# Odd mixer of a two-layer block: the last convolution chunk on VectorE instead of TensorE

## What is computed

```python
def sparse_attn_conformer_mixer(h, ...):
    u = h @ w_in
    ...
    o_nsa = native_sparse_attention(...)        # 8 heads of 64, 256 tokens
    a, b = jnp.split(cf, 2, axis=-1)            # 512 channels each
    z = a * jax.nn.sigmoid(b)
    z = causal_dwconv(z, conf_dw) + conf_dw_b   # depthwise, 31 taps over time
    z = jax.nn.silu(layer_norm(z, conf_ln_g, conf_ln_b))
    return jnp.concatenate([o_nsa, z], axis=-1) @ w_out
```

## Time and profile before

| | us |
|---|---|
| median of 3 runs | 1068.94 |
| lowest and highest run | 1055.47, 1072.68 |
| profiled execution, its own time | 1060.81 |
| its span in the trace | 1059.0 |
| PE busy, share of the span | 95% |
| DVE busy, share of the span | 59% |
| granted TensorE clock, mean | 0.982 |

### The profile page before, as it was taken

How to read it: one execution, slowest core, us unless ns; L and a number is a source line. 1 busy time by engine, 2 the same in 40 slices (tenths; PEclk the granted TensorE clock), 3 DMA queues, 4 the chain that set the end, 5 groups by cost and what they waited for, 6 DMA issues and landing times.

```text
span 1059.0 us, 16632 instructions
## 1 busy us (share of the span) xinstructions
PE 1010.6 (95%) x6822; PEld 902.1 (85%) x6822; DVE 620.1 (59%) x817; ACT 495.5 (47%) x723; POOL 198.6 (19%) x183
## 2 busy tenths in 40 slices
PE   5999999999998999999999999999999999699998
PEld 5988999999797789799999997777777778699996
DVE  4755554554688678665444546555755555646664
ACT  5346344344544443563344346454445544445452
POOL 0005950000222140000000001605253306200100
PEclk9999999999999699999999999999999999899999
DMA  8554665556584130346565564545453536263361
GB/s 270 191 179 145 211 199 170 190 194 195 144 257 160 49 112 2 99 154 190 194 198 170 189 236 143 175 127 166 128 190 122 158 105 200 80 199 119 110 210 40
DMA packets 120418, 168.69 MB, mean 159 GB/s; under 512 B 6372, under 2 KB 89508, under 8 KB 120356
## 3 DMA queue, kind: packets, MB, share of 16 engines
q1 hardware_dynamic: 119920, 167.65, 49.1%
q10 hardware_dynamic: 436, 0.19, 0.1%
HBM read 165.36 MB, written 2.46 MB: 158 GB/s over the span
## 4 chain that ended last, share of the span: by engine, by line
PE 88%; DVE 4%; ACT 3%; POOL 2%; issue 2%; DMA 1%; SPq 0%; DVEq 0%; ACTq 0%; POOLq 0%
PE ps L410 25%; PE ps L411 24%; PE ps L412 24%; PE ps L773 3%; PE ps L761 2%; PE ps L747 2%; PE ps L447 1%; PE ps L591 1%; ACT scratch_sb L811 1%; PE ps L457 1%; PE ps L450 1%; DVE wlo_sb L399 1%; PE ps L824 1%; DMA scratch_sb<-conf_dw 1%; POOL b_inv_sb L2204 1%
## 5 line engine op out<-in xcount | busy, mean ns | idle before, releaser
L399 DVE TENSOR_TENSOR wlo_sb<-raw_sb,whi_sb 128x2048 fp32r<-128x2048 f32 x150 | 345.7, 2306 | 201.2 <-ACT whi_sb L393 201.2
L393 ACT ACTIVATE whi_sb<-raw_sb 128x2048 fp32r<-128x2048 f32 x150 | 287.1, 1915 | 172.9 <-PE ps L412 161.2
L410 PE MATMUL ps<-hhi_sb,whi_sb 128*128 128x256 f32 x1024 | 289.4, 283 | 9.3 <-DVE qkl_sb L2090 7.2
L411 PE MATMUL ps<-hlo_sb,whi_sb 128*128 128x256 f32 x1024 | 287.6, 281 | 0.0
L412 PE MATMUL ps<-hhi_sb,wlo_sb 128*128 128x256 f32 x1024 | 287.3, 281 | 0.0
L410 PEld LDWEIGHTS ps<-hhi_sb,whi_sb 128*128 128x128 f32 x1024 | 194.4, 190 | 12.0 <-DVE wlo_sb L399 7.4
L411 PEld LDWEIGHTS ps<-hlo_sb,whi_sb 128*128 128x128 f32 x1024 | 194.5, 190 | 0.9
L412 PEld LDWEIGHTS ps<-hhi_sb,wlo_sb 128*128 128x128 f32 x1024 | 194.3, 190 | 0.0
L410 PE MATMUL ps<-whi_sb,hhi_sb 128*128 128x512 f32 (+1 forms) x304 | 120.2, 395 | 0.0
L410 PE MATMUL ps<-whi_sb,yhi_sb 128*128 128x512 f32 (+1 forms) x288 | 113.7, 395 | 3.4 <-issue 2.8
L412 PE MATMUL ps<-whi_sb,hlo_sb 128*128 128x512 f32 (+1 forms) x304 | 116.6, 383 | 0.0
(11 more groups left out here) (304 smaller groups left out, 1417.9 us busy)
## 6 DMA issues: line engine op xcount, KB each, us to landing
raw_sb<-w_in SPq DMA_DIRECT2D x45, 1024.0 KB, 5.2
raw_sb<-ffn_gate SPq DMA_DIRECT2D x22, 1024.0 KB, 5.3
raw_sb<-ffn_up SPq DMA_DIRECT2D x22, 1024.0 KB, 5.3
raw_sb<-ffn_down SPq DMA_DIRECT2D x22, 1024.0 KB, 4.9
raw_sb<-w_in_odd SPq DMA_DIRECT2D x9, 1024.0 KB, 5.2
raw_sb<-w_in_even SPq DMA_DIRECT2D x8, 1024.0 KB, 7.1
raw_sb<-w_branch SPq DMA_DIRECT2D x6, 1024.0 KB, 5.1
scratch_sb<-bias_rows_dram SPq DMA_DIRECT2D x40, 128.0 KB, 2.9
```

The lines of the kernel that those rows point to most:

```text
L393: nc.scalar.activation(whi[:, n0 % SPLIT, :], raw[:, n0 % RAW, :], ACT.Copy).then_inc(hi_ready, 1)
L399: nc.vector.tensor_tensor(wlo[:, n0 % SPLIT, :], raw[:, n0 % RAW, :], whi[:, n0 % SPLIT, :].bitcast(F32), ALU.subtract).then_inc(lo_ready, 1)
L410: nc.tensor.matmul(dst, l_hi, r_hi, start=first, stop=False)
L411: nc.tensor.matmul(dst, l_hi, r_lo, start=False, stop=False)
```

## The change

All 31 taps of chunk 3 go to DVE. The list of `conf_taps` now alternates between chunks 2 and 3 as it does between 0 and 1, with 4 taps at every step from 14 on. The products of `conv3` on PE, the splits of z for it on ACT and DVE, the diagonals on POOL, the splits of the tap weights (L2308, L2413) and `conv3_rest` are gone. PE's wait ahead of `channel_mean` is now for all 124 taps.

```diff
-PE_TAPS = 28
...
-        CONF_STEP, Z_STEP, ZH_STEP, ZL_STEP = (12, 13), 14, 15, 16
+        CONF_STEP, Z_STEP = (12, 13), 14
...
-                if m in CONV3_STEP:
-                    k = 2 * CONV3_STEP.index(m)
-                    if k == 0:
-                        pe.wait_ge(z_ready, 4)
-                        pe.wait_ge(z3_lo, 1)
-                        pe.wait_ge(diag_ready, 2 * PE_TAPS)
-                    conv3((k, k + 1))
...
-            pe.wait_ge(conf_step, 3 * CONF_K)
-            pe.wait_ge(conv3_step, CONF_K - PE_TAPS + 1)
+            pe.wait_ge(conf_step, 4 * CONF_K)
             channel_mean(zc, T)
...
-                    k, c = (s // 2, s % 2) if s < 2 * CONF_K else (s - 2 * CONF_K, 2)
+                    k, c = s % (2 * CONF_K) // 2, s // (2 * CONF_K) * 2 + s % 2
...
-                        dve.wait_ge(conf_step, s if c == 2 else s - 1)
+                        dve.wait_ge(conf_step, s - 1)
...
-                if m == ZL_STEP:
-                    dve.wait_ge(z3_hi, 1)
-                    nc.vector.tensor_tensor(zl, zp[:, 3, :], zh.bitcast(F32), ALU.subtract).then_inc(z3_lo, 1)
...
-                if m == CONV3_REST:
-                    conf_taps(3 * CONF_K, 3 * CONF_K)
-                    conv3_rest()
                 if m not in LO_STEP:
-                    conf_taps(2 if m % 2 == 0 else 3, (2 if m < Z_STEP else 3) * CONF_K)
+                    conf_taps((2 if m % 2 == 0 else 3) if m < Z_STEP else 4, (2 if m < Z_STEP else 4) * CONF_K)
...
-            for k in range(PE_TAPS):
-                nc.gpsimd.tensor_scalar(dgh[k], ident[:, :], dwh[:, k:k + 1].bitcast(F32), None,
-                                        ALU.mult).then_inc(diag_ready, 1)
-                nc.gpsimd.tensor_scalar(dgl[k], ident[:, :], dwl[:, k:k + 1].bitcast(F32), None,
-                                        ALU.mult).then_inc(diag_ready, 1)
```

More of the change, by code:

```diff
@@ L155, in build @@
         kcTl = sb("kcTl", [P, 16], F32R)
-        dwh = sb("dwh", [P, PE_TAPS], F32R)
-        dwl = sb("dwl", [P, PE_TAPS], F32R)
         gwhi = sb("gwhi", [P, KC, 24], F32R)
@@ L296, in build @@
         unit_r, hide_r = (t[:, :, :].rearrange("p k n -> p (k n)") for t in (gwhi, gwlo))
[L299 to L305, removed]
         bias_dram = nc.dram_tensor("bias_rows_dram", (H_TOT, SKEW_ROWS, DREL), F32, kind="Internal").ap()
@@ L354, in build @@
         hide_set = sem("hide_set")
-        dw_hi, dw_lo, diag_ready, z3_hi, z3_lo, conv3_done, conv3_step = (
-            sem("dw_hi"), sem("dw_lo"), sem("diag_ready"), sem("z3_hi"), sem("z3_lo"), sem("conv3_done"),
-            sem("conv3_step"))
         kv_twice, rot_ready, roped, kc_roped, kc_heads_T, u_scaled = (
@@ L897, in build @@
         FIN_STEP, OC_SUM_STEP, SUM_STEP, OT_STEP = (18, 30), (22, 31), 26, 31
-        GROUP_STEP, CONV3_REST = (8, 16, 24), 30
-        STEPS1, CONV3_STEP = range(-2, 33), range(17, 31)
+        GROUP_STEP = (8, 16, 24)
+        STEPS1 = range(-2, 33)
         def mix1_pe(pe):
@@ L969, in out_rows @@
                 mm_rows(n, yhi, ylo, k0, first, last).then_inc(tile_used, 1)
[L971 to L976, removed]
             def cmp_part(row, k0, k1):
@@ L1203, in mix1_act @@
                         pair_copy_act(act, jobs1, 0, p, 0, 2)
[L1204 to L1207, removed]
                 if m in HID_STEP:
@@ L2271, in _ @@
             pool.wait_ge(ident_landed, 16)
-            pool.wait_ge(dw_hi, 1)
-            pool.wait_ge(dw_lo, 1)
-            pool.wait_ge(x_added, 4)
-            for k in range(PE_TAPS):
-                nc.gpsimd.tensor_scalar(dgh[k], ident[:, :], dwh[:, k:k + 1].bitcast(F32), None,
-                                        ALU.mult).then_inc(diag_ready, 1)
-                nc.gpsimd.tensor_scalar(dgl[k], ident[:, :], dwl[:, k:k + 1].bitcast(F32), None,
-                                        ALU.mult).then_inc(diag_ready, 1)
             norm_pool(pool, 2)
@@ L2306, in _ @@
                                          ps[:, t, :], ACT.Copy).then_inc(c_copied, 1)
-            act.wait_ge(half_set, 1)
-            nc.scalar.activation(dwh[:, :], dwv[:, 0:PE_TAPS, 3], ACT.Copy).then_inc(dw_hi, 1)
             act.wait_ge(pool_mm, 1)
@@ L2411, in _ @@
             split_lo(dve, N_MIX0 + 10)
-            dve.wait_ge(dw_hi, 1)
-            nc.vector.tensor_tensor(dwl[:, :], dwv[:, 0:PE_TAPS, 3], dwh[:, :].bitcast(F32),
-                                    ALU.subtract).then_inc(dw_lo, 1)
             gate(1)
```

## The result

The changed kernel takes 1073.34 us in the median of 20 runs (1067.51 to 1080.44); the kernel before, on the same chip, takes 1059.96 us in the median of 20 (1053.73 to 1077.3). The ratio is 1.0131, with a 95% interval of 1.0111 to 1.0150: slower by 12 to 16 us. The forecast of the time, 1075 us, lay close for a poor reason: its base, the median of three runs, was 9 us too high, and its effect, +6 us, was about half of the least that the change costs and less than half of the 13 to 14 us measured. Two errors of opposite sign met; that is luck.

A forecast was written before the change was run, and what follows sets the result against it. The prediction took PE to bound the stage, DVE next; DVE's queue (+3 us) and a low clock over one long pair (+3 us) gave +6 us on the 1068.9 us median, so 1075 us, range 1060 to 1084 us.

The forecast's parts named there:

- the third case: Clock stays low from 388 us to the stage's end and PE is the bound again: +12 us, chance 0.15.
- the first: Forecast case: DVE's queue sets the stage (+3 us), clock low over one long PE pair (+3 us): +6 us, chance 0.45.
- PE bounds the kernel before, DVE is next: Stage from 388.81 to 424.53 us: PE busy 35.72 of 35.72 us, DVE 30.57, or 86%.
- The price of the taps: DVE from step 14: taps in turn cost 0.41 us, chained 0.51; the queue grows by 7.3 us.
- Its waits of 3.8 us absorb part: DVE's waits for scores and `conv3` fill with the added taps, leaving net +3.5 us, taken as +3.
- The mean, "nothing is added": First channel mean, waiting for all 124 taps, still ends with DVE's last three operations; 1.95 us, nothing added.
- The clock term, +3 us over one long pair: Low clock over one of two pairs with L1083: 8.0 us on PE against DVE's 4.5, +3.5, of which 3 kept.
- The second case, DVE's queue alone, +3 us: DVE's queue alone sets the stage, clock up for most of it: +3 us, chance 0.28.
- POOL's diagonals nil: Removing POOL's 56 diagonals from 93.70 us on wins nothing; at most 0.54 us of PE's time could come back.
- POOL's sums beside the taps "in both sums": POOL's weighted sums from 393.60 us slow DVE's taps by 2.2 us before and after alike, so it cancels.
- The other side, not slower: DVE hides more, at a tap price of about 0.36 us instead of 0.41: -1 us, chance 0.09.
- The median: Forecast's base: median of three runs, 1068.94 us, with the profiled execution 8.1 us below it.

The follow-up runs named there:

- exp. 12: Kernel before's PE queue kept, its 84 `conv3` products unread, with the changed kernel's DVE queue of all 124 taps; 1071.59 us against 1060.43 us, ratio 1.0085.
- experiment 11: Kernel before with only the three `conv3_rest` taps taken in turn with the third chunk's first three; 1059.62 us against 1059.89 us, ratio 1.0010.
- experiment 3: Kernel before without the 84 `conv3` products, nothing in their place, 28 taps left out of the result; 1067.97 us against 1062.16 us, ratio 1.0033.
- experiment 10: Changed kernel with ten idle PE products in each of fourteen steps, 140 in all; 1073.67 us (four runs), ratio 1.0146.
- experiment 4: Changed kernel with POOL's 56 diagonals and the splits of the tap weights kept but unread; 1075.35 us, ratio 1.0111.
- experiment 9: Kernel before with 20 instead of 28 last-chunk taps on PE and the other eleven on DVE, no fillers; 1067.72 us, ratio 1.0056.

## Why the prediction was right or wrong

Its sum for the stage against what the profiled executions show, in us over the kernel before:

```
                                  forecast   changed   exp. 12
DVE's own work                    +7.3       +7.45     +7.74
DVE's waits                       -3.8       +2.2      -1.8
the mean and what hangs on it      0         +2.7      +1.65
clock low over a long pair        +3         in the two above
sum                               +6 (rounded)  +12.4  +7.6
```

The forecast took 7.3 - 3.8 = 3.5 us as +3; no row gives the 0.5 us. In experiment 12 the clock is up from 400 to 433 us only, and mostly at 0.50 while the mean runs.

- **By its own signs the third case came, not the first.** The mean began 10.2 us later and not 2 to 7, the waits for L828 (now L812) were the long ones that the forecast had called the sign of being wrong, and the clock up to 424.53 us was 0.50 and not near 0.75. The third case, put on the same base, would have said 1081 us.
- **PE bounds the kernel before, DVE is next**: right. Each of DVE's three waits in its stretch, 3.79 us in all, ends with PE, and experiment 11 gave DVE 0.2 us less to do and moved nothing.
- **The price of the taps**: right. 0.405 us in turn against 0.41 forecast, and the queue's own work +7.45 us against +7.3. From what the Trainium skill says in VectorE: DVE Perf Modes, section The DRAIN you can't avoid (a chain costs the same with a semaphore after each operation as without), the forecast inferred that chained and alternating taps might cost alike; the rows stay on the other side, 0.51 and 0.405 us.
- **"Its waits of 3.8 us absorb part: with PE lighter by 10.4 us, the scores are there when DVE comes for them"**: this step did not hold. I treated idle time as a pool that longer work drains, and counted the discount at the full clock while forecasting a low one. The waits came to 6.0 us: 3.29 us behind the sixteen small products, which is the forecast's own clock term (3.5 us for that pair), 2.39 us behind the small scores of L1036, and 0.33 us. The forecast left none of them, so that is 6.0 us against it, of which the clock term gives 3 back. In experiment 12, with the clock up at both places, 2.0 of the 3.8 us stayed, but beside the 84 products that the change takes away. No run has PE lighter and the clock up, so whether the step would hold there is not shown.
- **The mean, "nothing is added"**: wrong by 2.7 us in the changed kernel and 1.65 us in experiment 12, where the clock was low at that place too. Before, the mean started 2.6 us ahead of the end of DVE's last sum; now it starts 1.9 us ahead of it, after PE has waited for the last tap, and takes 3.69 us because the clock is low. I priced it at the upper level while forecasting a low clock.
- **The clock term, +3 us over one long pair**: mis-sized in its reach, not in its price. One long pair at 0.50 cost 7.89 us on PE (397.89 to 405.78) against 8.0 forecast, and the wait behind it 3.29 us against 3.5. But the clock was at 0.50 over the whole stretch of 388.81 to 424.53 us, as the third case had it, and so the pair with the small scores, which the forecast held to be free of the clock, cost another 2.39 us. The third case gave 46.8 us from 388.8 us to the mean and 12 us in all; the trace has 45.89 us and 12.4 us. So near a hit is partly chance: the case had PE full throughout and L1066 unchanged at 1.4 us, while PE was busy 42.34 us, with gaps and with the clock back from 424.5 to 428 us, and L1066 rose to 2.58 us. The case was given 0.15. The reason that I set against it, that a PE without a gap would be lifted again, is refuted by experiment 3 and by the after trace from 400 to 424 us; in experiment 10 a full PE lost the upper level and got it back. The row that spoke for it, 342.88 to 363.44 us at 0.50 with PE 19.89 of 20.56 us busy, was the better witness.
- **The second case, DVE's queue alone, +3 us**: too low. In experiment 12, with the clock up from 400 to 433 us, the queue costs 7.6 us in the trace, and in executions as they come 9 us, with a lower mean clock.
- **POOL's diagonals nil**: nothing speaks against it (experiment 4, which tells 4 us). **POOL's sums beside the taps "in both sums"**: nearly. Eight taps from 394.71 us take 5.84 us against 3.24 us undisturbed, 2.6 us lost against the 2.2 of before.
- **The other side, not slower**: not borne out; the taps cost 0.405 us, not 0.36.
- **The median**: of the three runs shown (1055.47, 1068.94 and 1072.68 us) two lie where only a third of the later executions do, at 1066 to 1076 us; the others lie at 1054 to 1064 us. The some 10 us between are the clock's, 0.985 against 0.973. The spread of the three runs, wider than the effect, was in the table, and the forecast took it for scatter. The profiled execution, 1060.81 us, lay within 1 us of the median of twenty.

## What to carry to other kernels

Idle time of an engine that gets more work is no discount: see which wait it is and whether what ends it will come sooner, and count only that. Work taken from a full TensorE may slow what is left of it; make the sum at both clock levels, with every term of it, the short tail included, before giving chances. Put the mean granted clock beside every execution's time before reading a difference of one per cent, and split a move into "taken away alone" and "added alone": each half costs one run and they needn't be what the whole suggests.

## What was not expected of the hardware

- The clock stayed at 1.2 GHz with PE busy without a gap: in experiment 3 from 404 to 444 us (4.00 of 4.00 us in each of ten stretches), in the changed kernel from 400 to 424 us, in experiment 9 from 404 to 416 us. In experiment 10 it fell from 1.00 to 0.50 in such a stretch, at about 404 us, and was back at 1.00 by 412 us. The Trainium skill's TensorE: Matmul & The Clock Gate, section HAM oscillation, ties throttling to long idleness; here a gap came first in some cases (384 to 396 us of the changed kernel) and in experiment 10 the profile shows hardly one in the 12 us ahead of the fall (3.97 of 4.00 us busy, then 4.00 twice).
- Taking 84 products from PE didn't make the kernel measurably faster (ratio 1.0033, 0.9991 to 1.0074), and putting 84 idle ones into the changed kernel made it 3 us faster by the medians, 6.6 us by the ratios. Fillers ahead of the stage came with a higher clock there and a longer fall behind, 4.7 us gained and 4.7 us lost in the two traces compared.
- The mean clock explains the scatter of a kernel's executions to within 0.3 to 1.0 us, with 0.5 to 1.1 us of time for 0.001 of clock, by kernel.

What stays open: why the same kernel draws one of two levels of mean clock, in which stretch its slower executions lose it (the kernel before was profiled only in a faster one), and why six fillers per step held the clock for most of the stage where three didn't and ten did no better. Nor was it shown what the change would cost with the clock up and nothing put in the products' place. No version was measured to be faster than the kernel before.
